# Two attention stages of a two-block transformer: dense pieces dealt in halves, a projection begun inside the attention, a division moved to GpSimd

## The chip, the cores and the metric

The kernel runs on one core of one Trainium2 chip. The metric is device time in microseconds, the median over executions; less is better. An engine is named by its short name in rows: PE is TensorE, DVE VectorE, ACT ScalarE, POOL GpSimd, SP the queue that issues loads.

## What is computed

512 tokens of width 1024 pass two transformer blocks in float32. The first block's attention has two halves whose results are concatenated and projected by `w_o`:

```python
o_nsa = nsa_attention(q_n, k_cmp, v_cmp, k_slc, v_slc, k_win, v_win, gates, nsa_slopes)
o_swa = swa_attention(q_s, k_s, v_s, sinks, swa_slopes)
mix = jnp.concatenate([o_nsa, o_swa], axis=-1) @ w_o
x = x + rmsnorm(mix, attn_post_g)
```

A gated MLP with a short convolution follows (`w_gate_up`, `w_down`), then a gated embedding term. The second block has a neighbourhood attention (8 heads) beside a retention, `w_out`, and an MLP:

```python
s = jnp.where(valid, s + bias, NEG)
p = jax.nn.softmax(s, axis=-1)
out = jnp.einsum('bhcqij,bicjhd->bcqhd', p, v_win)
x = x + jnp.concatenate([na_out, ret_out], axis=-1) @ w_out
x = x + jnp.square(jax.nn.relu(rms_norm(x, norm_mlp) @ w_up)) @ w_down
```

## The kernel before

Every engine has its own program, written out by hand, and waits on semaphores. No scheduler reorders anything.

**Dense products.** A float32 product is made of three matmuls (`triple`, lines 593 to 595): high weight by high input, high by low, low by high. A weight comes in pieces of 128x512. SP loads piece i into one of five `raw` buffers, ScalarE makes its high part `wh` (L1323), VectorE (L2022) or GpSimd (L2943) its low part `wl`, into one of five pairs. So the high part of piece i+5 waits until TensorE has finished piece i. A piece against 512 tokens is 12 matmuls with 512 columns.

**First attention.** 28 units run through a pipeline of 31 steps: units 0 to 7 are sliding window, units 8, 13, 18 and 23 the compressed branch, the others selected and window branches in turn. In step s each engine does, in this order:

- TensorE: dense pieces given to the step by `FILL1`; transpositions of unit s-2 (`turn1`, L813, or L854 for a compressed unit); scores of unit s+1 (`scores1`, L799 and L800, or L843); values of unit s-3 (`values1`, L826 and L827, L866 for the compressed part).
- VectorE: scaling of the dense piece that ended (`filled`, L2095 and L2097), mask and minimum of unit s (`soft1`, L2191), sum of the two heads of an output (`out_add`, L2214), its low part (`out_low`, L2219), low parts of the probabilities of unit s-3 (`rest1`, L2207), reciprocal for unit s-1 (`norm1`, L2272), then low parts of queries or keys (`filled_low`, L2104, L2105, L2109).
- ScalarE: copies that a finished dense piece asks for (`filled`; for a `w_o_swa` piece the copy `acc<-bank`, L1533), exponent of unit s (L1510), `wh` of a later piece, high parts of the transposed probabilities (L1516), copy of an output (L1521).
- GpSimd: division of unit s-1 with its gate (`norm1`, L2969, four instructions), then low parts of weights (L2943).

**Banks.** PSUM has eight banks. `Banks` hands them out first in, first out: `take` gives the one free for longest, and the taker waits until whoever read its former content is done. Scores, transpositions, outputs and dense results all take from this one list.

**Behind the attention.** The projection of the selected half, `w_o_nsa`, has eight pieces with four inputs each. The fourth input is the last output of the attention. `behind_last` computes inputs 0 to 2 of the first two pieces after step 30, and then input 3 of both; pieces 2 to 7 follow. As each of the eight results comes, VectorE adds it (`y1`, L2344), makes a low weight part, and adds squares for the norm (L2086). SP's queue waits for the values of the last unit, loads two quarters of `X` (L3059), waits for `y1(2)`, loads the other two, and then `praw` (L3060), which ScalarE turns into `PH` (L1601) in turn between two squares, and VectorE into `PL` (L2363). TensorE's norm sums (L724) wait for the sixth addition of squares.

**Neighbourhood attention.** Eight units, ten steps. TensorE: scores of unit s+1, values of s-2, transpositions of s-1, then one or two dense pieces (`FILL2`). VectorE: `soft` (L2191), `rest` (L2207), then `norm`, the reciprocal (L2198) and four multiplications (L2202, 1280 columns in all), then work on dense results and outputs.

## Time and profile before

| | |
|---|---|
| median of 3 runs | 1287.24 us (1286.85 to 1287.76) |
| profiled execution, its own time | 1286.42 us |
| its span, first to last instruction | 1284.5 us |
| TensorE busy | 1263.0 us, 98% |
| VectorE busy | 786.6 us, 61% |
| ScalarE busy | 647.9 us, 50% |
| GpSimd busy | 216.9 us, 17% |
| mean granted TensorE clock | 0.996 |

The profiled time is 0.8 us under the median, and its span 1.9 us under its own time. Busy shares are means over stages. The first attention's steps run from about 72 to 228 us, its projection to 250 us, the neighbourhood attention from about 827 to 895 us. In a timeline of TensorE the length given beside a matmul reaches into the next one; what a matmul costs is the distance between starts, about 0.23 us for one with 512 columns at full clock.

### The profile page before, as it was taken

How to read it: one execution, taken by the hardware profiler on the slowest of the kernel's cores; microseconds unless marked ns; L12 is line 12 of the kernel's file. 1: busy time of each engine (PE TensorE's matmuls, PEld its weight loads, DVE VectorE, ACT ScalarE, POOL GpSimd, SP SyncE). 2: the span in 40 equal slices, each digit the busy share in tenths (PEclk: the TensorE clock that was granted, in tenths of full speed). 3: DMA queues.
4: the chain of work that ended last, by engine and by line, in shares of the span. 5: the costliest groups of instructions: out<-in, count | busy, mean ns of one | idle time of the engine just before them, and what ended most of it. 6: DMA issues, size and time to landing. Idle time of an engine off the chain costs nothing.

```text
span 1284.5 us, 16448 instructions
## 1 busy us (share of the span) xinstructions
PE 1263.0 (98%) x6004; PEld 1045.6 (81%) x6004; DVE 786.6 (61%) x1465; ACT 647.9 (50%) x1261; POOL 216.9 (17%) x234
## 2 busy tenths in 40 slices
PE   9999999999999999999999999999999999999998
PEld 8887888878888888888787777887888888888887
DVE  6689687686645565356788876589644343343334
ACT  6787788554335433233555655586533252332344
POOL 0064555000100011001002101032311030110111
PEclk9998999999999999999999999999999999999999
DMA  7211110423333323332333212432333324233332
GB/s 275 86 50 34 42 41 26 170 82 99 90 100 98 98 90 99 99 96 68 115 91 98 76 56 68 131 112 68 98 99 92 97 75 118 79 115 89 100 90 67
DMA packets 64626, 118.20 MB, mean 92 GB/s; under 512 B 7713, under 2 KB 12193, under 8 KB 64289
## 3 DMA queue, kind: packets, MB, share of 16 engines
q1 hardware_dynamic: 62704, 112.86, 29.3%
q10 hardware_dynamic: 1840, 4.29, 1.1%
q8 instruction: 48, 0.79, 0.3%
q14 instruction: 34, 0.27, 0.1%
HBM read 115.02 MB, written 2.10 MB: 91 GB/s over the span
## 4 chain that ended last, share of the span: by engine, by line
PE 90%; DVE 4%; ACT 2%; issue 2%; DMA 1%; POOL 1%; POOLq 0%; SPq 0%; DVEq 0%; ACTq 0%
PE bank L593 26%; PE bank L595 25%; PE bank L594 25%; PE bank L813 2%; PE bank L693 2%; PE bank L694 2%; PE bank L695 2%; PE bank L826 1%; PE bank L827 1%; PE bank L799 1%; PE bank L800 1%; PE bank L767 1%; DVE q2p L2191 0%; DMA praw<-in_pT 0%; DVE r_bc L2086 0%
## 5 line engine op out<-in xcount | busy, mean ns | idle before, releaser
L2022 DVE TENSOR_TENSOR wl<-raw,wh 128x512 fp32r<-128x512 f32 (+2 forms) x360 | 267.5, 754 | 325.5 <-ACT wh L1323 324.8
L1323 ACT ACTIVATE wh<-raw 128x512 fp32r<-128x512 f32 (+1 forms) x398 | 242.2, 618 | 284.7 <-PE bank L595 273.7
L593 PE MATMUL bank<-AH,wh 128*128 128x512 f32 (+1 forms) x848 | 333.8, 394 | 2.1 <-DVE AL L2036 0.8
L595 PE MATMUL bank<-AH,wl 128*128 128x512 f32 (+1 forms) x848 | 329.3, 388 | 0.0
L594 PE MATMUL bank<-AL,wh 128*128 128x512 f32 (+1 forms) x848 | 327.0, 386 | 0.0
L593 PE MATMUL bank<-BH,wh 128*128 128x512 f32 x624 | 247.7, 397 | 1.6 <-ACT acc L1533 1.6
L595 PE MATMUL bank<-BH,wl 128*128 128x512 f32 x624 | 244.6, 392 | 0.0
L594 PE MATMUL bank<-BL,wh 128*128 128x512 f32 x624 | 243.0, 389 | 0.0
L595 PEld LDWEIGHTS bank<-AH,wl 128*128 128x128 f32 x848 | 159.6, 188 | 35.8
L593 PEld LDWEIGHTS bank<-AH,wh 128*128 128x128 f32 x848 | 159.9, 189 | 35.2 <-issue 2.9
L594 PEld LDWEIGHTS bank<-AL,wh 128*128 128x128 f32 x848 | 159.7, 188 | 33.0 <-issue 0.2
L593 PEld LDWEIGHTS bank<-BH,wh 128*128 128x128 f32 x624 | 117.3, 188 | 27.7 <-ACT acc L1533 2.1
L595 PEld LDWEIGHTS bank<-BH,wl 128*128 128x128 f32 x624 | 117.2, 188 | 27.2
L594 PEld LDWEIGHTS bank<-BL,wh 128*128 128x128 f32 x624 | 117.2, 188 | 25.6 <-issue 0.5
L2985 POOL TENSOR_TENSOR BL<-tmp,BH 128x512 fp32r<-128x512 f32 x22 | 28.6, 1300 | 354.4 <-ACT BH L1632 354.4
L3013 POOL TENSOR_TENSOR AL<-tmp,AH 128x512 fp32r<-128x512 f32 x32 | 40.6, 1303 | 269.6 <-ACT AH L1954 269.6
L2943 POOL TENSOR_TENSOR wl<-raw,wh 128x512 fp32r<-128x512 f32 x38 | 50.2, 1323 | 100.2 <-ACT wh L1323 100.2
L1510 ACT ACTIVATE pp<-pp,small 128x128 f32<-128x128 f32 (+2 forms) x96 | 50.2, 525 | 7.5 <-DVE small L2191 7.1
L2969 POOL TENSOR_SCALAR pp<-pp,small,gates 128x128 f32<-128x128 f32 (+1 forms) x64 | 40.9, 654 | 34.2 <-DVE small L2272 34.2
L2805 DVE TENSOR_TENSOR X<-X,bank 128x512 f32<-128x512 f32 x46 | 31.5, 686 | 24.3 <-PE bank L595 24.2
L2869 DVE SCALAR_TENSOR_TENSOR tmp<-bank,r_bc 128x512 f32<-128x512 f32 x32 | 22.0, 691 | 27.6 <-PE bank L595 16.1
L2191 DVE CUSTOM_DVE_ANT_0 pp<-bank,dn 128x512 f32<-128x512 f32 (+1 forms) x64 | 27.5, 486 | 15.9 <-PE bank L800 15.7
(332 smaller groups left out, 1617.4 us busy)
## 6 DMA issues: line engine op xcount, KB each, us to landing
raw<-in_w_dn SPq DMA_DIRECT2D x104, 256.0 KB, 2.7
raw<-in_w_gu SPq DMA_DIRECT2D x88, 256.0 KB, 2.6
raw<-in_w_up SPq DMA_DIRECT2D x64, 256.0 KB, 2.6
raw<-in_w_nsa SPq DMA_DIRECT2D x16, 256.0 KB, 2.7
raw<-in_w_pg SPq DMA_DIRECT2D x16, 256.0 KB, 2.7
raw<-in_w_naq SPq DMA_DIRECT2D x16, 256.0 KB, 2.7
nbi<-in_na_bias ACTq DMA_DIRECT2D x8, 448.0 KB, 3.4
raw<-in_w_swa SPq DMA_DIRECT2D x10, 256.0 KB, 2.7
```

The source lines that it names most:

```text
L593: t.matmul(o, w, xh, start=start, stop=False, skip_group_check=skip)
L594: t.matmul(o, w, xl, start=False, stop=False, skip_group_check=skip)
L595: return t.matmul(o, wl, xh, start=False, stop=stop, skip_group_check=skip)
L1323: a.activation(W[i % NW].h[:, 0:n], RAW[i % NRAW][:, 0:n], ACT.Copy).then_inc(*s_wh.up(i))
L1510: m = a.activation(o, o, ACT.Exp, bias=m4[:, qb:qb + 1], scale=-1.0, accum_out=s4[:, qb:qb + 1])
L2022: v.tensor_tensor(w.l[:, 0:n], RAW[i % NRAW][:, 0:n], w.h[:, 0:n], ALU.subtract).then_inc(*s_wl.up(i))
L2191: m = v.tensor_tensor_reduce(o, b[:, col:col + w], bias(qb), scale, init, ALU.add, ALU.min, m4[:, qb:qb + 1])
L2805: v.tensor_tensor(chunk(X, c), chunk(X, c), bank.ap(key)[:, :], ALU.add).then_inc(*s_sv.up(done))
L2943: g.tensor_tensor(w.l[:, 0:n], RAW[i % NRAW][:, 0:n], w.h[:, 0:n], ALU.subtract).then_inc(*s_wlg.up(i))
L2969: g.tensor_scalar(o, o, r, by, ALU.mult, ALU.mult).then_inc(*s_nmg.up((u, qb)))
L2985: g.tensor_tensor(x.l, tmp.ap(("u", k))[:, 0:T], x.h, ALU.subtract).then_inc(*s_xlg.up(("ff", k)))
L3013: g.tensor_tensor(x.l, tmp.ap(("rs", 8 * gi + k))[:, 0:T], x.h, ALU.subtract).then_inc(*s_xlg.up(("up", 8 * gi + k)))
```

## The change

Three edits.

1. **First attention's dense pieces.** The table `FILL1` becomes `PARTS1`, which gives a piece to a step whole (`ALL`), or its first or last two inputs (`FRONT`, `BACK`). `part` takes these halves. `("w_nsa", 3)`, the second half of the window keys, moves from step 8 to step 7, which had none; query pieces `("w_nsa", 10)` to 13 begin a step earlier; pieces 14 and 15 are spread over steps 13 to 16, the `w_o_swa` pieces over steps 16 to 27 rather than in 13, 14, 18, 21, 23, 26 and 27. `FILL1` is kept as the table of where a piece ends, and the other engines follow it.
2. **The projection.** `out_front` computes inputs 0 to 2 of one piece; it is called in steps 28, 29 and 30, ahead of the values, and once behind step 30. `out_back` computes input 3, for pieces 0 to 3 one after the other; whole pieces 4 to 7 follow. The neighbourhood attention's `w_out_na` uses the same functions in the order it had.
3. **The division.** `norm` leaves VectorE. Its reciprocal for unit s-1 now stands at the head of VectorE's step s, ahead of `soft`; the four multiplications are on GpSimd, with a second factor of one, ahead of its low weight parts. TensorE's transpositions wait for GpSimd's semaphore.

```diff
-FILL1 = {0: [("w_swa", 6), ("w_swa", 7)], 1: [("w_swa", 8)], 2: [("w_nsa", 0), ("w_swa", 9)], 3: [("w_nsa", 1)],
-         4: [("w_nsa", 8)], 5: [("w_nsa", 9)], 6: [("w_nsa", 2)], 8: [("w_nsa", 3)], 9: [("w_nsa", 10)],
-         10: [("w_nsa", 11)], 11: [("w_nsa", 12)], 12: [("w_nsa", 13)], 13: [("w_o_swa", 0)],
-         14: [("w_o_swa", 1), ("w_o_swa", 2)], 15: [("w_nsa", 14)], 16: [("w_nsa", 15)], 18: [("w_o_swa", 3)],
-         21: [("w_o_swa", 4)], 23: [("w_o_swa", 5)], 26: [("w_o_swa", 6)], 27: [("w_o_swa", 7)]}
+ALL, FRONT, BACK = (0, 1), (0,), (1,)
+PARTS1 = {0: [("w_swa", 6, ALL), ("w_swa", 7, ALL)], 1: [("w_swa", 8, ALL)], 2: [("w_nsa", 0, ALL), ("w_swa", 9, ALL)],
+          3: [("w_nsa", 1, ALL)], 4: [("w_nsa", 8, ALL)], 5: [("w_nsa", 9, ALL)], 6: [("w_nsa", 2, ALL)], 7: [("w_nsa", 3, ALL)],
+          8: [("w_nsa", 10, ALL)], 9: [("w_nsa", 11, ALL)], 10: [("w_nsa", 12, ALL)], 11: [("w_nsa", 13, FRONT)],
+          12: [("w_nsa", 13, BACK)], 13: [("w_nsa", 14, FRONT)], 14: [("w_nsa", 14, BACK)], 15: [("w_nsa", 15, FRONT)],
+          16: [("w_nsa", 15, BACK), ("w_o_swa", 0, FRONT)], 17: [("w_o_swa", 0, BACK), ("w_o_swa", 1, FRONT)],
+          18: [("w_o_swa", 1, BACK)], 19: [("w_o_swa", 2, FRONT)], 20: [("w_o_swa", 2, BACK), ("w_o_swa", 3, FRONT)],
+          21: [("w_o_swa", 3, BACK)], 22: [("w_o_swa", 4, ALL)], 23: [("w_o_swa", 5, FRONT)], 24: [("w_o_swa", 5, BACK)],
+          25: [("w_o_swa", 6, ALL)], 26: [("w_o_swa", 7, FRONT)], 27: [("w_o_swa", 7, BACK)]}
+FILL1 = {s: [(name, i) for name, i, h in parts if 1 in h] for s, parts in PARTS1.items()}
...
+            def out_front(name, c, src, ready, key):
+
+                b, free = bank.take((key, c))
+                w, i = weights(name, c)
+                e.wait_ge(*free)
+                for k in range(3):
+                    e.wait_ge(ready(k))
+                    col = slice(P * k, P * k + P)
+                    triple(b[:, :], w.h[:, col], src[k].h, src[k].l, w.l[:, col], k == 0, False)
...
+                if s >= N_UNITS:
+                    out_front("w_o_nsa", s - N_UNITS, B, nsa_out, "wo")
                 if s >= 3:
                     values1(s - 3)
...
-            behind_last("w_o_nsa", B, nsa_out, "wo")
-            for c in range(2, 8):
+            out_front("w_o_nsa", 3, B, nsa_out, "wo")
+            for c in range(4):
+                out_back("w_o_nsa", c, B, nsa_out, "wo")
+            for c in range(4, 8):
                 product("w_o_nsa", c, B, nsa_out, [0, 1, 2, 3], 1, 4, [("wo", c)])
...
             for s in range(10):
+                if 1 <= s <= 8:
+                    s4 = S4[(s - 1) % 6]
+                    e.wait_ge(s_ex.at(("na", s - 1)))
+                    v.reciprocal(s4, s4).then_inc(*s_nm.up(("r", ("na", s - 1))))
                 if s < 8:
...
-                if 1 <= s <= 8:
-                    norm(NA, ("na", s - 1), PP2[(s - 1) % 2], S4[(s - 1) % 6])
...
+            def norm(L, u, pp, s4, by):
+                e.wait_ge(s_nm.at(("r", u)))
+                for qb in range(4):
+                    o = pp[:, L["off"][qb]:L["off"][qb] + L["w"][qb]]
+                    g.tensor_scalar(o, o, s4[:, qb:qb + 1], by(qb), ALU.mult, ALU.mult).then_inc(*s_nmg.up((u, qb)))
...
-            for s in range(10):
-                for name, i in FILL2.get(s, ()):
+            for s in range(1, 11):
+                if s <= 8:
+                    norm(NA, ("na", s - 1), PP2[(s - 1) % 2], S4[(s - 1) % 6], one)
+                for name, i in FILL2.get(s - 1, ()):
                     lo(WHERE[name, i] + 4)
```

How the order moves on the engines, at three places. Line numbers behind the change are those of its own code.

VectorE in the first attention, where the low parts of the window keys (`kb_wn`) are made. Before, at the end of step 9, behind the compressed unit's division:

```order
L2260 TENSOR_REDUCE small<-pc 128x8
L2262 RECIPROCAL small<-small 128x8
L2264 TENSOR_TENSOR small<-small,gates 128x8
L2266 TENSOR_TENSOR pc<-pc,small 128x2x4x31
L2104 TENSOR_TENSOR kb_wn_95<-tmp_74,ka_wn_94 64x512
L2105 TENSOR_TENSOR kb_wn_95<-tmp_74,ka_wn_94 64x512
L2104 TENSOR_TENSOR kb_wn_97<-tmp_74,ka_wn_96 64x512
L2105 TENSOR_TENSOR kb_wn_97<-tmp_74,ka_wn_96 64x512
L2191 ISA pp_111,small<-bank,dn 128x512
```

Now at the end of step 8, behind the small compressed values (`vc`), and ahead of the mask of unit 9:

```order
L2276 TENSOR_TENSOR small<-small 128x4
L2278 RECIPROCAL small<-small 128x4
L2334 TENSOR_TENSOR vc_104<-bank,vc_104 31x64 x2
L2334 TENSOR_TENSOR vc_105<-bank,vc_105 31x64 x2
L2118 TENSOR_TENSOR kb_wn_95<-tmp_74,ka_wn_94 64x512
L2119 TENSOR_TENSOR kb_wn_95<-tmp_74,ka_wn_94 64x512
L2118 TENSOR_TENSOR kb_wn_97<-tmp_74,ka_wn_96 64x512
L2119 TENSOR_TENSOR kb_wn_97<-tmp_74,ka_wn_96 64x512
L2205 ISA pp_115,small<-bank,dn 128x512
```

The four low parts moved up by one step, ahead of the mask of unit 9 instead of that of unit 10.

TensorE in step 29, from the transpositions of the last unit on. Before, the values of unit 26 follow at once:

```order
L813 MATMUL bank<-ident,pp_115 128x128 x10
L866 MATMUL bank<-pct,vc_105 128x512
L826 MATMUL bank<-pth_107,v_100 128x512
L827 MATMUL bank<-ptl_108,v_100 128x512
L826 MATMUL bank<-pth_107,v_101 128x384
```

Now the front of projection piece 1 stands between (nine matmuls, the first five shown):

```order
L818 MATMUL bank<-ident,pp_115 128x128 x10
L598 MATMUL bank<-BH,wh_60 128x512
L599 MATMUL bank<-BL,wh_60 128x512
L600 MATMUL bank<-BH,wl_61 128x512
L598 MATMUL bank<-BH,wh_60 128x512
L599 MATMUL bank<-BL,wh_60 128x512
```

Steps 28 and 30 have the same for pieces 0 and 2, so 27 matmuls moved ahead of the last values.

VectorE in the neighbourhood attention, step 2. Before, the division stands between the low parts of the probabilities and the scaling of a dense result:

```order
L2207 TENSOR_TENSOR p2l_161<-bank,p2h_160 128x512
L2207 TENSOR_TENSOR p2l_161<-bank,p2h_160 128x384 x2
L2198 RECIPROCAL small<-small 128x4
L2202 TENSOR_SCALAR q2p_165<-q2p_165,small 128x256
L2202 TENSOR_SCALAR q2p_165<-q2p_165,small 128x384 x2
L2202 TENSOR_SCALAR q2p_165<-q2p_165,small 128x256
L2095 TENSOR_TENSOR tmp_74<-bank,r_bc 128x512
```

Now the scaling follows at once:

```order
L2213 TENSOR_TENSOR p2l_161<-bank,p2h_160 128x512
L2213 TENSOR_TENSOR p2l_161<-bank,p2h_160 128x384 x2
L2109 TENSOR_TENSOR tmp_74<-bank,r_bc 128x512
L2711 TENSOR_TENSOR nkb_184<-tmp_74,nka_183 64x512
L2712 TENSOR_TENSOR nkb_184<-tmp_74,nka_183 64x512
```

and GpSimd has the multiplications ahead of its low weight parts:

```order
L2972 TENSOR_SCALAR q2p_164<-q2p_164,small,ones 128x256
L2972 TENSOR_SCALAR q2p_164<-q2p_164,small,ones 128x384 x2
L2972 TENSOR_SCALAR q2p_164<-q2p_164,small,ones 128x256
L2951 TENSOR_TENSOR wl_59<-raw_51,wh_58 128x512
L2951 TENSOR_TENSOR wl_61<-raw_52,wh_60 128x512
```

## Rows read from the trace of the kernel before

**Rows 1.** The page, busy time by engine (share of the span, instructions).

```profile
PE 1263.0 (98%) x6004; PEld 1045.6 (81%) x6004; DVE 786.6 (61%) x1465; ACT 647.9 (50%) x1261; POOL 216.9 (17%) x234
```

**Rows 2.** TensorE's waits, 96 to 245 us: total us, times, longest us.

```profile
PE bank L813 <- ACT acc L1533: 2.9, 3, 1.3
PE bank L593 <- ACT acc L1533: 1.6, 2, 1.3
PE bank L799 <- issue: 1.6, 1, 1.6
PE bank L813 <- POOL pp L2969: 1.1, 2, 0.6
```

**Rows 3.** TensorE's timeline, steps 7 and 8: start us, length, instruction, [idle before, releaser].

```profile
101.04 1.51 PE L813 MATMUL bank<-ident,pp 128*128 128x128 f32 x6 [0.64 <-POOL pp L2969]
102.94 0.33 PE L790 MATMUL bank<-cw,chid 128*64 128x64 f32 x2 [0.39 <-DVE os L2214]
...
107.58 0.63 PE L595 MATMUL bank<-AH,wl 128*128 128x512 f32 x1
108.00 0.63 PE L593 MATMUL bank<-AH,wh 128*128 128x512 f32 x1
...
110.36 0.39 PE L593 MATMUL bank<-AH,wh 128*128 128x512 f32 x1
110.59 0.39 PE L594 MATMUL bank<-AL,wh 128*128 128x512 f32 x1
```

**Rows 4.** TensorE's timeline, window keys in step 9.

```profile
119.27 0.47 PE L799 MATMUL bank<-ka_wn,qs 128*128 128x512 f32 x1 [1.58 <-issue]
```

**Rows 5.** By stretch: length, busy PE, PEld, DVE, ACT, POOL (x), clock, DMA.

```profile
105.10:137.18 32.08, 30.50 (x172) 26.69 (x173) 28.62 (x76) 25.26 (x68) 15.25 (x21) 0.92 0.13 38
836.00:896.00 60.00, 58.21 (x321) 48.96 (x321) 54.01 (x137) 44.76 (x107) 17.13 (x13) 1.00 0.31 94
```

**Rows 6.** ScalarE's timeline, steps 13 and 14.

```profile
144.94 0.59 ACT L1521 ACTIVATE os<-bank 64x512 f32<-64x512 f32 x1 [1.85 <-PE bank L827]
145.56 0.60 ACT L1533 ACTIVATE acc<-bank 128x512 f32<-128x512 f32 x1
```

**Rows 7.** Chain that ended last, 237 to 251 us: start us, us, what.

```profile
236.81 0.70 DVE ACC L2344
...
238.38 5.71 DMA praw<-in_pT
...
244.11 0.64 ACT PH L1601
...
249.85 0.70 DVE r_bc L2086
...
250.69 0.41 PE bank L724 x2
```

**Rows 8.** VectorE's timeline: the attention's last output, first projection result.

```profile
230.57 0.69 DVE L2219 TENSOR_TENSOR BL<-os,BH 128x512 fp32r<-128x512 f32 x1 [0.70 <-ACT BH L1525]
233.38 0.69 DVE L2344 TENSOR_TENSOR ACC<-bank,acc 128x512 f32<-128x512 f32 x1 [2.12 <-PE bank L595]
```

**Rows 9.** Timelines of the neighbourhood attention: TensorE, then VectorE and GpSimd.

```profile
868.40 0.39 PE L799 MATMUL bank<-nka,nq 128*128 128x256 f32 x1 [1.05 <-DVE os L2214]
870.73 0.35 PE L826 MATMUL bank<-p2h,v 128*128 128x256 f32 x1 [0.55 <-DVE p2l L2207]
...
860.27 1.27 DVE L2202 TENSOR_SCALAR q2p<-q2p,small 128x256 f32<-128x256 f32 x4
866.07 1.68 DVE L2219 TENSOR_TENSOR AL<-r_bc,AH 128x512 fp32r<-128x512 f32 x1
...
865.51 1.68 POOL L2943 TENSOR_TENSOR wl<-raw,wh 128x512 fp32r<-128x512 f32 x1 [2.14 <-ACT wh L1323]
```

**Rows 10.** GpSimd's timeline, divisions of the first attention's wide units.

```profile
136.29 2.38 POOL L2969 TENSOR_SCALAR pp<-pp,small,gates 128x128 f32<-128x128 f32 x4 [2.27 <-DVE small L2272]
141.92 3.30 POOL L2969 TENSOR_SCALAR pp<-pp,small,gates 128x128 f32<-128x128 f32 x4 [1.99 <-DVE small L2272]
```

More of the change, by code:

```diff
@@ L641, in product, with part @@
                         group(name, k0 + s // kpp, bs, keys, src, ready, ks[s:s + kpp], s == 0, s + kpp == n, fresh is not None)
-            def part(name, k, src, ready, ks, key, first, last, between=None):
-                if first:
+            def part(name, k, src, ready, ks, key, first, last, between=None, halves=ALL):
+                if first and 0 in halves:
                     b, free = bank.take(key)
@@ L649, in part @@
                 w, i = weights(name, k)
-                for j in range(4):
+                for j in range(2 * halves[0], 2 * halves[-1] + 2):
                     x = src[ks[j]]
@@ L1216, in na_out @@
                 return s_xl.at(("ob", "na", k))
-            behind_last("w_out_na", A, na_out, "xo")
+            for c in range(2):
+                out_front("w_out_na", c, A, na_out, "xo")
+            for c in range(2):
+                out_back("w_out_na", c, A, na_out, "xo")
             for c in range(2, 8):
@@ L2194, in soft @@
                     bank.read(("sc", u, i), (s_sf, ("b", u, i)))
-            def norm(L, u, pp, s4):
-                e.wait_ge(s_ex.at(u))
-                v.reciprocal(s4, s4).then_inc(*s_nm.up(("r", u)))
-                e.wait_ge(s_nm.at(("r", u)))
-                for qb in range(4):
-                    o = pp[:, L["off"][qb]:L["off"][qb] + L["w"][qb]]
-                    v.tensor_scalar(o, o, s4[:, qb:qb + 1], None, ALU.mult).then_inc(*s_nm.up((u, qb)))
             def rest(L, u, pt, before):
@@ L2958, in gpsimd, with one @@
             g.memset(chid[1][:, :], 0.0).then_inc(*s_z.up("zero"))
+            def norm(L, u, pp, s4, by):
[3 more added lines that the diff above has]
+                    g.tensor_scalar(o, o, s4[:, qb:qb + 1], by(qb), ALU.mult, ALU.mult).then_inc(*s_nmg.up((u, qb)))
+            def one(qb):
+                return ones[:, 0:1]
             def norm1(u):
[L2961 to L2964 removed]
+                if unit(u)[0] == "swa":
+                    norm(SWA, u, probs(u), S4[u % 6], one)
+                else:
                     e.wait_ge(s_dv.at("gv"))
[L2966 to L2969 removed]
+                    norm(NSA, u, probs(u), S4[u % 6], lambda qb: gate_of(u)[:, qb:qb + 1])
             for s in range(1, N_UNITS + 3):
```

44 lines of the change are left out of this document (14 added, 30 removed).

## The prediction

> **What bounds the kernel now.** I read busy time by engine first: TensorE is busy 1263.0 of 1284.5 us [rows 1]. The change adds and removes no matmul; only TensorE's waits and its slow clock can go, so 21 us of idle and the little that the clock costs are all there is. TensorE's waits of the first attention come next [rows 2]. Three kinds matter: 4.5 us on `acc`, the copy of a `w_o_swa` result out of its bank; 1.6 us ahead of the window keys' scores; 1.1 us on GpSimd's division. The timeline shows more than the waits do, since matmul lengths there overlap the next start. In step 7, with no dense piece, the seven transpositions of unit 5 began at 100.07 and what followed them at 102.94 [rows 3]; elsewhere such a group takes 0.7, so 2.2 were lost. Behind that thin stretch the granted clock fell to its lower level, 1.2 GHz: starts of 512-column matmuls stand 0.42 apart at 107.58, and 0.23 again at 110.36 [rows 3]. The slow stretch begins behind 102.94 and ends ahead of 110.36, 6.9 us at half speed by the starts, 3.4 lost. The scores at 119.27 had TensorE idle for 1.58 [rows 4], 1.8 by starts. The stretches show who stands behind this: from the mask of unit 8 to that of unit 13 (105.10 to 137.18) VectorE is busy 28.62 of 32.08, and in the neighbourhood attention 54.01 of 60 [rows 5].
>
> **First attention, steps 7 to 13.** The removed stalls are 2.2 + 3.4 + 1.8 = 7.4 us, and that is the upper end. TensorE could do less: from its 30.50 busy us [rows 5] the new table takes one piece out of steps 8 to 12 (12 x 0.23 = 2.7), and the slow clock inflated them by some 2.5, so it needs 25.3. VectorE needs the same 28.6, and its work can hardly start earlier: with `w_nsa` 3 in step 7, TensorE reaches unit 8's scores at about 103.8 instead of 103.2, now at full clock, and the mask starts at 105.05 instead of 105.10. So VectorE sets the pace, and TensorE waits for it in small portions. If it idles 1.4 us in handovers instead of 3.5, unit 13's mask comes at 135.1 instead of 137.18: lead 2.1, the lower end. Placing the steps one by one with the durations of the rows, TensorE enters step 13 at 134.5 instead of 138.3, with the same pieces done; it waits less behind VectorE's last work. I take **3.8**, nearest to this placement. The window keys are no wait any more: their low parts are ready at 114.2, wanted at 114.6.
>
> **First attention, steps 13 to 27.** A result's bank is taken again as the next step's first bank, while ScalarE copies the ended unit's output (0.59) and only then `acc` (0.60) [rows 6]: 1.3 us wherever an output ended in that step, 0.3 elsewhere. Following the list of banks, five such waits (1.3, 1.3, 1.3, 0.3, 0.3) become three (step 19 behind `w_o_swa` 1, 1.3; steps 22 and 25, 0.3); the others meet a `BACK` half, which takes no bank. That gives 4.5 - 1.9 = **2.6**, between 0 (all come back elsewhere, as VectorE's read of a score bank in step 17 might) and 4.5. Sum of the first attention 6.4.
>
> **Projection.** In steps 28 to 30 the fronts (9 x 0.23 = 2.07 each) fill the 1.0 us that TensorE lost on GpSimd's last division (the 1.1 of rows 2). Against that, front 1 takes the bank of an output read 1.5 us after its values, 0.5 lost; and only front 3 (2.07) now stands between the last values and input 3, which came 2.9 us after them (the first matmul behind the values started at 228.35, the low part ended at 231.26) [rows 8], 0.85 lost. Before, two fronts of 4.1 covered it. So TensorE ends the eight pieces no earlier, 29.7 us after step 28 began as against 29.6.
>
> What matters is what comes late. The first result came at 233.38 [rows 8], 12.6 us into this stretch; now four come in a bunch, from 16.7 on. VectorE takes them one by one: result, low part, result, low part, squares, result, some 4.0 us to the end of `y1(2)`, at 20.7 instead of 16.6. On `y1(2)` SP's queue releases the second half of `X` and then `praw`, which needed 5.71 us from issue to landing, and on which ScalarE waited [rows 7]. From its landing at 244.11 a chain of VectorE and ScalarE work without a gap led to the last addition at 249.85 and to TensorE's norm sums at 250.69 [rows 7]; TensorE had finished its pieces at 250.4, so nothing was to spare. The transfer carries 1.5 MB, and nothing in the change makes that shorter. So the whole chain moves by 4.05, and TensorE stands idle about 4 us ahead of the norm sums: **-4.0**, between 0 (if `praw` lands early) and -4.5.
>
> An idle stretch like this costs clock too. In step 7 a stretch with 2.2 of 2.9 us idle was enough for the fall, which cost 3.4 [rows 3]. Here it would meet norm sums and embedding matmuls, part of them hidden behind VectorE: I take **-2.0**, between 0 and -3.4.
>
> **Neighbourhood attention.** VectorE gives up four multiplications of 1.27 together, eight times [rows 9]; GpSimd takes 2.38 to 3.30 for 1280 columns in the first attention [rows 10], and had been busy 17 of 60 us here [rows 5]; its 8 x 2.4 to 3.3 = 19 to 26 us fit. The division starts before the mask instead of behind it and the probabilities' low parts (2.0 + 1.6), so it is done at about 2.7 to 3.5 us into VectorE's step instead of 5.1. TensorE's path there is VectorE: at 868.40 it waited for an output sum, at 870.73 for low parts [rows 9]. Idle, by that view, is 1.8 of 60 [rows 5]; by starts it is more, as in step 7: 132 dense matmuls at 0.23 and 22 groups of scores, values and transpositions of 1.0 to 1.2 make 55.3 of the 60.5 us from 835.0 to 895.5, so 5.2 are lost. Relieved of 1.27 per step of 6 to 9 us, VectorE falls below TensorE: I take **+4.2**, between 0.5 and 5.2. The reciprocal now waits for ScalarE's exponent with the next mask behind it; 3.0 us of low parts, additions and sums stand between mask and reciprocal, the exponent takes 2.2, so it costs nothing.
>
> A rule speaks against this edit. The Trainium skill, GPSIMD Engine Reference, section "Key points", says that GpSimd shares its SBUF interfaces with VectorE, and that they contend when VectorE reads two SBUF inputs. The trace agrees: `AL`, 0.69 elsewhere, took 1.68 at 866.07 beside a GpSimd subtraction begun at 865.51 [rows 9]. Whether a division, with one input, does as much no row tells here; that is the third rival.
>
> **Sum.** 3.8 + 2.6 + 0 - 4.0 - 2.0 + 4.2 = 4.6 us from the profiled 1286.4, so 1281.8. The median stood 0.8 higher: 1287.2 - 4.6 = 1282.6, rounded **1282.5**.
>
> **Rivals.** (A) The tail has no wait: `praw` lands in time, or the chain is shorter than I hold. Then 10.6 are gained, **1276.6**. For it: VectorE had idle stretches before `y1(4)`; against: ScalarE's wait for the transfer is in the chain. (B) VectorE's pace swallows steps 7 to 13, and one `acc` wait returns: 2.1 + 1.3 - 6.0 + 4.2 = 1.6, **1285.6**. (C) Slower: GpSimd's added work holds up VectorE's two-input operations. With four per step at up to 1 us, 1.27 saved per step can be outweighed; it decides from one and a half collisions per step. Then the neighbourhood attention gives 0.5 at best or loses 2, and with the pace of B and the full fall of the clock in the tail: 2.1 + 1.3 - 7.4 - 2 = -6, **1293**. (D) The halves do not do what they say: TensorE's waits move to score banks in steps 17 and 20 and to the divisions, which have 1.4 instead of 2.7 us of cover. First attention gains 2 in all: 2 - 6 + 4.2 = 0, **1287**.
>
> **How the numbers follow.** My forecast has 0.45, A 0.17, B 0.14, C 0.12, D 0.12. 0.2% of the time, 2.6 us, is about what a measurement of this kernel can tell from none; so faster means under 1284.7. The forecast lies there for nine tenths, A whole, B a third: 0.63. Slower is C: 0.11. The rest, 0.26, is within. The range leaves out half of A's low side and most of C: 1276.5 to 1288.
>
> **What would show it.** Right: no idle at about 100 to 103 and no slow clock behind it; no wait ahead of the window keys; one `acc` wait of 1.3 and two of 0.3; VectorE busy over 90% in steps 8 to 12; about 4 us idle before the norm sums (L729 then), with `praw` in the chain and landing some 27 us behind step 28's transpositions; the neighbourhood attention's TensorE waits under 0.5. Wrong, if the norm sums wait under 1 us, if the clock falls in steps 9 to 14, or if VectorE's low parts of keys take over 1 us beside GpSimd's divisions.

## The result and the profile after

| | before | changed |
|---|---|---|
| median | 1287.05 us (4 runs, 1286.27 to 1287.76) | 1301.87 us (4 runs, 1299.92 to 1302.81) |
| ratio, 95% interval | | 1.0113 [1.0098, 1.0128] |
| profiled execution, its span | 1286.42, 1284.5 | 1302.53, 1300.7 |

The change made the kernel 14.8 us slower. The forecast was 4.6 faster; the time lies outside its range and 9 us above its slowest rival.

The page's busy times of the changed kernel, to compare with [rows 1]:

```profile
PE 1267.9 (97%) x6004; PEld 1050.6 (81%) x6004; DVE 782.5 (60%) x1433; ACT 647.6 (50%) x1261; POOL 236.3 (18%) x266
```

The work is the same; TensorE is busy 4.9 us longer, with a mean granted clock of 0.992 instead of 0.996, and idle 11 us longer. Its waits from 96 to 262 us, against [rows 2] (total us, times, longest us):

```profile
PE bank L729 <- DVE r_bc L2100: 5.4, 1, 5.4
PE bank L598 <- ACT acc L1547: 3.5, 2, 2.2
PE bank L818 <- DVE vc L2334: 2.8, 1, 2.8
PE bank L818 <- POOL pp L2972: 1.4, 4, 0.4
PE bank L848 <- DVE ptl L2213: 1.4, 1, 1.4
PE bank L818 <- DVE os L2220: 0.9, 2, 0.5
PE bank L831 <- DVE ptl L2213: 0.7, 1, 0.7
PE bank L598 <- DVE BL L2225: 0.7, 1, 0.7
PE bank L598 <- DVE os L2220: 0.4, 1, 0.4
```

Of five waits for `acc` two are left, where three were forecast, but one of them takes 2.2 us, and behind that one the granted clock fell, which it did nowhere in these steps before:

```profile
185.00:206.00 21.00, 18.76 (x109) 16.03 (x108) 12.65 (x38) 14.93 (x44) 10.86 (x15) 0.92 0.14 39
```

The wait ahead of the window keys is gone. In their place stand waits on banks that VectorE reads (`vc`, `ptl`, `os`), and 5.4 us ahead of the norm sums. The same stretches as [rows 5], placed by the same masks and steps (length, busy PE, PEld, DVE, ACT, POOL, clock, DMA):

```profile
107.30:138.70 31.40, 26.30 (x159) 22.30 (x158) 29.01 (x74) 25.35 (x67) 16.85 (x20) 1.00 0.14 43
848.00:908.00 60.00, 55.64 (x302) 47.95 (x301) 47.92 (x106) 44.44 (x109) 32.35 (x40) 0.94 0.29 87
```

In the first TensorE's need fell from 30.5 to 26.3 us, at full clock, and yet the stretch is only 0.7 shorter. In the second VectorE is 6 us less busy and GpSimd 15 more, and TensorE, whose clock fell, does fewer matmuls in 60 us.

Both traces, cut at the same instructions of TensorE:

| stretch | before | changed | difference | forecast |
|---|---|---|---|---|
| start to the 7th step's dense piece or transpositions | 100.1 | 101.8 | +1.8 | 0 |
| to step 13 | 38.3 | 37.7 | -0.6 | -3.8 |
| to step 28 | 82.4 | 83.7 | +1.2 | -2.6 |
| to the norm sums | 29.9 | 37.1 | +7.2 | +4.0 |
| to the neighbourhood attention's start | 576.5 | 579.1 | +2.65 | +2.0 |
| to the end | 457.4 | 461.3 | +3.9 | -4.2 |

Every row but the first was a term of the sum; plus is slower here. All five came out worse, the fourth by little.

### The profile page after: what moved, and what is told of

Read it like the earlier page. It is cut to its first block, busy times and chain, and to the rows that moved or that the text cites. A ratio compares the mean times of both kernels' runs of the same rounds, so it can differ in the third digit from the quotient of the medians.

```text
span 1300.7 us, 16451 instructions
## 1 busy us (share of the span) xinstructions
PE 1267.9 (97%) x6004; PEld 1050.6 (81%) x6004; DVE 782.5 (60%) x1433; ACT 647.6 (50%) x1261; POOL 236.3 (18%) x266
## 4 chain that ended last, share of the span: by engine, by line
PE 87%; DVE 6%; ACT 3%; issue 2%; DMA 1%; POOL 0%; SPq 0%; POOLq 0%; DVEq 0%; ACTq 0%
PE bank L598 25%; PE bank L600 24%; PE bank L599 24%; PE bank L698 2%; PE bank L699 2%; PE bank L700 2%; PE bank L818 2%; PE bank L831 1%; PE bank L832 1%; PE bank L804 1%; PE bank L805 1%; ACT q2p L1524 1%; DMA raw<-in_w_ple 1%; DVE q2p L2205 1%; PE bank L772 1%
## 5 line engine op out<-in xcount | busy, mean ns | idle before, releaser
L2811 DVE TENSOR_TENSOR X<-X,bank 128x512 f32<-128x512 f32 x46 | 31.5, 687 | 24.8 <-PE bank L600 24.7
L2972 POOL TENSOR_SCALAR pp<-pp,small,ones 128x256 f32<-128x256 f32 (+1 forms) x32 | 22.1, 703 | 80.0 <-DVE small L2278 80.0
```

What stands on the lines that cost most here:

```text
L2811: v.tensor_tensor(chunk(X, c), chunk(X, c), bank.ap(key)[:, :], ALU.add).then_inc(*s_sv.up(done))
L2972: g.tensor_scalar(o, o, s4[:, qb:qb + 1], by(qb), ALU.mult, ALU.mult).then_inc(*s_nmg.up((u, qb)))
```

## The experiments

Each kernel below was compared with the kernel before on one chip, in five rounds (`d0_before` ran once). A distance "8 to 13" is from the first compressed score of unit 8 to that of unit 13, the tail is from step 28 to the norm sums.

### The three edits alone

The diff of each is the part of the change that its name says, on the kernel before.

`a1_table`:

> The kernel before with the new table of dense pieces alone (PARTS1 and halves in part); projection and division as before. Theory T (the losses stand in separate stages and add): the two traces differ by +0.6 us from step 7 to step 28 where the removed stall of step 7 was to give 6; so this kernel comes out within 1.5 us of the kernel before (1286 to 1289), with a wait of 2 to 3 us of the transpositions in step 8 for VectorE's read of the compressed values, and none in step 7. Rival R (the table is sound, its gain is eaten by the other two edits): 1281 to 1283.

`a2_proj`:

> The kernel before with the projection's fronts in steps 28 to 30 alone. Theory T: the tail of the first attention and its norm carry +7.2 and +2.65 us of the loss by the two traces; so 1295 to 1298, with an idle stretch of 5 us ahead of the norm sums and a granted clock that falls behind it. Rival R (the old table leaves the tail's transfers early enough, the loss comes only with the new table's late pieces of w_o_swa): 1287 to 1291. Rival C (the prediction's size): 4.05 + 2 us, 1293.

`a3_div`:

> The kernel before with the neighbourhood attention's division on GpSimd alone, reciprocal at the head of VectorE's step. Theory T: +3.9 us by the two traces, so 1290 to 1292. Rival N (this stage's loss in the trace of the change was inherited from what stood ahead of it): 1283 to 1287.

| | median, before beside it (us) | ratio, interval | 8 to 13 | 13 to norm sums | norm sums to neighbourhood attention | to the end |
|---|---|---|---|---|---|---|
| before | | | 32.9 | 114.6 | 576.5 | 457.4 |
| changed | 1301.87, 1287.05 | 1.0113 [1.0098, 1.0128] | 31.5 | 123.1 | 579.1 | 461.3 |
| `a1_table` | 1290.16, 1287.91 | 1.0022 [1.0013, 1.0031] | 31.5 | 118.0 | 576.6 | 457.4 |
| `a2_proj` | 1294.69, 1287.91 | 1.0054 [1.004, 1.0067] | 32.9 | 119.0 | 579.0 | 457.4 |
| `a3_div` | 1290.53, 1287.91 | 1.0026 [1.0016, 1.0035] | 32.9 | 115.0 | 576.4 | 460.9 |

No edit gains, each loses in the stage that it touches, and the losses add: 2.3 + 6.8 + 2.6 = 11.7 of 14.8 by the medians. By the spans, less what each trace shows ahead of step 7's first instruction (next experiment), it is 3.0 + 6.9 + 4.1 = 14.0 of 14.4. `a1_table` came out 1.2 us above what theory T gave it, `a2_proj` 0.3 under, nearer to T than to C (1293). The rivals by which an edit was sound by itself fall. The table has two losses. Between 13 and 28 it is 1.3 us slower, with the same wait of 2.2 us for `acc` in step 22 and a fall of the clock behind it at 191.1 us, as in the changed kernel. And its tail is 32.0 against 29.9: behind half a piece in steps 26 and 27, instead of a whole one, TensorE waits 1.0 us for GpSimd's divisions and 0.7 for VectorE's low parts, where it waited 0.4 and nothing. These two readings come from the waits; no run changed either place by itself.

### What the traces differ by before any changed instruction

`d0_before`:

> The kernel before once more, for a second profile. In the traces so far TensorE's clock rises at either of two points at the start of the program, and unit 8's scores begin at 103.2 to 103.8 or at 104.8 to 105.1 us. Theory L (this is the execution's luck and no effect of an edit): this one may show either, and its own time is 1285.5 to 1286.5 with the early and 1287.5 to 1289 with the late one, everything behind in the same distances. Rival K (each kernel has its own): the early one again.

It took 1288.3 us, and its unit 8 began at 104.8 instead of 103.2. TensorE's timeline at the start, in the first profile of the kernel before and then in this one (start us, length, instruction):

```profile
5.66 0.99 PE L680 MATMUL bank<-wh,AH 128*128 128x408 f32 x4 [1.04 <-ACT wh L1323]
6.48 0.91 PE L683 MATMUL bank<-wh,AL 128*128 128x408 f32 x4
```

```profile
5.68 1.70 PE L680 MATMUL bank<-wh,AH 128*128 128x408 f32 x4 [0.87 <-ACT wh L1323]
7.18 1.56 PE L683 MATMUL bank<-wh,AL 128*128 128x408 f32 x4
```

The same four matmuls take 0.8 us or 1.5, from start to start: the clock rises earlier or later, and in `d0_before` everything behind keeps its distances. The changed kernel's trace has the late rise too. So theory L holds, and 1.8 of the 16.2 us of span belong to the execution. It isn't the only such chance: in `e1_low_waits`, below, the clock fell once more at 765 us, 3.5 us after sixteen matmuls of one column each had begun, without a wait of TensorE and in code that no edit touches (length, busy PE, PEld, DVE, ACT, POOL, clock, DMA):

```profile
762.00:770.00 8.00, 8.00 (x37) 6.43 (x38) 5.22 (x19) 4.50 (x7) 0.00 (x0) 0.79 0.11 33
```

Its stretch from the norm sums to the neighbourhood attention took 578.1 us for that, not 576.5. So a difference of 1 or 2 us is read from the medians and from single stretches, not from the length of one trace.

### Steps 7 to 13

`a4_key7` moves one entry on the kernel before:

```diff
-6: [("w_nsa", 2)], 8: [("w_nsa", 3)], 9: [("w_nsa", 10)],
+6: [("w_nsa", 2)], 7: [("w_nsa", 3)], 9: [("w_nsa", 10)],
```

> The kernel before with one entry moved: the second half of the window keys in step 7 instead of 8, nothing in step 8. Theory T (the new table's loss is its query pieces begun a step early, which hand the transpositions of step 8 the bank of the compressed values; moving the one piece keeps step 7 busy and the clock up): 1281 to 1284. Rival V (VectorE sets the pace of these steps, whatever TensorE does): 1285 to 1287. Rival S (step 8 is now the thin one, and the stall and the clock's fall move there): 1286 to 1289.

1289.35, ratio 1.0015 [1.0006, 1.0024]. The stall of step 7 is gone, and in step 8 the scores of unit 9 wait for `vc`; 8 to 13 took 33.3:

```profile
111.93 0.80 PE L799 MATMUL bank<-ka_sl,qs 128*128 128x512 f32 x1 [5.04 <-DVE vc L2328]
```

It is nearest to rival S: the stall and the clock's fall moved to step 8. What S did not name is the cause, the list of banks: the key's bank comes back a step sooner, so another taker gets the bank of the compressed values, and VectorE reads that one last in its step. Here the taker is the scores of unit 9. In the changed kernel it is the transpositions of unit 6; TensorE's row and VectorE's:

```profile
113.87 0.55 PE L818 MATMUL bank<-ident,pp 128*128 128x128 f32 x3 [2.83 <-DVE vc L2334]
```

```profile
112.91 0.91 DVE L2334 TENSOR_TENSOR vc<-bank,vc 31x64 fp32r<-31x64 f32 x4 [0.49 <-ACT vc L1581]
```

`b1_key7_vc` adds, and `c1_table_vc` has on `a1_table`:

```diff
-                bank.give(("vc",))
...
+                if s == 8:
+                    bank.give(("vc",))
```

> The window keys' second half in step 7, and the bank of the compressed values given back to the list behind step 8's scores instead of at once. Theory T (in the kernel with the one piece moved, 5.0 us of idle stand in step 8 only because the transpositions of unit 6 get that bank, which VectorE reads at 111 us; all other steps run in the same distances): that wait goes, the slow clock behind it too, and the time falls by the 5 to 7 us that the old table lost at steps 7 to 9: 1281 to 1284. Rival V (VectorE sets the pace between the masks of unit 8 and 13): TensorE then waits elsewhere, 1285 to 1288.

> The new table alone, and the bank of the compressed values given back to the list behind step 8's scores. Theory T (the table's own losses are separate: 2.8 us of wait for that bank in step 8; 2.2 us of wait for ScalarE's copy of an output result in step 22; 2.1 us in the thinned last steps): 1287 to 1288.5, that is 1.5 to 3 us under the run with the table alone. Rival V (VectorE sets the pace in steps 8 to 12, the wait only moves): 1289.5 to 1290.5, no change.

`b1_key7_vc` gave 1287.84, ratio 1.0005 [0.9996, 1.0014]; `c1_table_vc` 1289.93, 1.0019 [1.001, 1.0028], as `a1_table`. The wait for `vc` went and others came: in `b1_key7_vc` TensorE waits 2.4 and 1.2 us for `os`, the sum of outputs on VectorE. Theory T falls in both, V stands. `d3_key_twice` gives more work to VectorE alone:

```diff
+                if key[1] == "wn":
+                    v.tensor_tensor(dst.l[half(g), 0:n], t[half(g), 0:n], dst.h[half(g), 0:n], ALU.subtract).then_inc(*s_ql.up((*key, g, "once")))
+                    e.wait_ge(s_ql.at((*key, g, "once")))
                 v.tensor_tensor(dst.l[half(g), 0:n], t[half(g), 0:n], dst.h[half(g), 0:n], ALU.subtract)
```

> The run with the keys in step 7 and the bank given later, where VectorE makes one low part of the window keys twice (twice 0.69 us or more, at the end of its step 8). Theory V (VectorE sets the pace between the masks of unit 8 and 13): the distance from unit 8's to unit 13's compressed scores grows from 31.6 to 33.0 or more, and the time from 1287.8 to 1289.2 to 1290. Rival E (TensorE's own waits set it, VectorE has 2.6 us idle there): 31.6 and 1287.8, no change.

1289.96, ratio 1.0019 [1.001, 1.0028]: 0.0014 over `b1_key7_vc`, 1.8 us for 1.4 us of added work. The two intervals overlap a little; but all eleven times of `d3_key_twice` (1289.1 to 1291.7) lie above all eleven of `b1_key7_vc` (1285.9 to 1288.5), with the kernel before at 1287.64 and 1287.22 beside them. Its waits of TensorE, 96 to 140 us:

```profile
PE bank L812 <- DVE os L2218: 4.0, 1, 4.0
PE bank L798 <- DVE os L2218: 1.2, 1, 1.2
```

These waits prove nothing by themselves: `d1_all`, below, has the same instructions in these steps as `b1_key7_vc`, without the added work, and waits 4.0 and 1.2 us as well. Nor do the distances 8 to 13: 31.6 in `b1_key7_vc`, 34.1 in `d1_all`, 34.8 in `d3_key_twice`. The clock differs between the three traces. In `b1_key7_vc` it was low once, ahead of the long wait (0.57 from 112 to 116 us); in `d1_all` at the wait and behind it (0.62, then 0.53, from 116 to 124), where it cost time; in `d3_key_twice` on both sides (0.68 from 112 to 116 and again from 120 to 124). So the times, over eleven runs each, decide for V over E; how much of the 1.8 us is the clock's stays open.

### The waits for acc

`c3_acc_early`, on the kernel before, ScalarE's program:

```diff
                 for name, i in later:
-                    filled(name, i)
+                    if name != "w_o_swa":
+                        filled(name, i)
...
+                for name, i in FILL1.get(s, ()):
+                    if name == "w_o_swa":
+                        filled(name, i)
                 if 3 <= s < N_UNITS + 3 and closes(s - 3):
```

> The kernel before, ScalarE copies the result of a w_o_swa piece (acc) in the step in which TensorE makes it, ahead of its copy of the ended unit's output, instead of behind it at the head of the next step. Theory A (TensorE's 4.5 us of waits for acc are real idle, as the prediction took them; 2.6 of them were a term of its sum): the waits vanish from the trace and the time falls by 2.5 to 4.5 us, 1282.7 to 1284.7. Rival P (TensorE is held by VectorE and GpSimd right behind, the wait only moves to the outputs' sum or the division): 1286 to 1287.5.

1286.76, ratio 0.9994 [0.9986, 1.0003]; 13 to norm sums 114.5 against 114.6. TensorE's waits, 96 to 245 us, against [rows 2]:

```profile
PE bank L799 <- issue: 1.6, 1, 1.6
PE bank L813 <- POOL pp L2973: 1.6, 4, 0.6
PE bank L813 <- DVE os L2218: 1.5, 2, 1.0
PE bank L790 <- DVE os L2218: 0.4, 1, 0.4
PE bank L854 <- DVE pc L2270: 0.4, 2, 0.2
```

All 4.5 us on `acc` are gone, and no gain can be told from none (by the interval at most 1.8 us). In step 14 TensorE came 1.6 us ahead. From step 19 on, which has no dense piece, it lost that bit by bit to GpSimd's division and VectorE's `os` (0.8 ahead at unit 22's scores, nothing at unit 27's). The `acc` waits had stood in front of those. That is rival P.

### The projection

`b2_proj_sp`, on `a2_proj`, SP's queue:

```diff
                 if c == 2:
+                    d.dma_start(praw[:, :], ins["pT"]).then_inc(*s_p.up("in", by=16))
+                    load(WHERE["w_ple", 1])
                     e.wait_ge(s_sv.at(("y1", 2)))
...
-            d.dma_start(praw[:, :], ins["pT"]).then_inc(*s_p.up("in", by=16))
```

> The projection's fronts alone, as in the run before, with SP's queue in another order: praw and the second piece of w_ple are issued ahead of the wait for y1(2), the second half of X behind it. Theory T (the projection's loss of 6.8 us is the chain y1(2), X, praw, w_ple, ScalarE, squares, norm sums): most of it goes, with it the idle stretch of 5 us ahead of the norm sums and the slow clock behind: 1287 to 1290. Rival B (the bunch of four results is itself what is late: eight additions, low parts and squares of VectorE from 241 us on): 1291 to 1294, the norm sums wait for VectorE at the same place. Rival D (the transfer is as slow wherever it is issued): no change against 1294.7.

1289.52, ratio 1.0013 [1.0004, 1.0022], 5.2 us under `a2_proj` by the medians and 3.9 by the two traces behind unit 8's first score. The wait ahead of the norm sums, first in `a2_proj`, then here:

```profile
PE bank L724 <- DVE r_bc L2095: 4.2, 1, 4.2
```

```profile
PE bank L724 <- DVE r_bc L2095: 1.2, 1, 1.2
```

Tail 34.3, 31.3, and 29.9 before. Theory T holds for three of the four microseconds of wait; the last 1.2 are rival B's: in this trace the chain ahead of the norm sums is VectorE's additions, low parts and squares, and no transfer. The changed kernel's chain of waits shows what lands last, against [rows 7]:

```profile
245.19 0.61 DVE ACC L2350
...
247.14 0.43 SPq L3076
...
247.61 7.98 DMA raw<-in_w_ple
255.62 0.64 ACT wh L1337
...
259.47 0.70 DVE r_bc L2100
...
260.31 1.73 PE bank L729 x7
```

It is not `praw` (5.71 us from issue to landing before, 6.24 now) but a load queued behind it, the second piece of `w_ple`: 7.98 us under way, where the trace of the kernel before has 6.64 for the same load. ScalarE makes its high part ahead of the sixth square. Behind the wait the clock is low:

```profile
264.71 0.63 PE L600 MATMUL bank<-PH,wl 128*128 128x512 f32 x1
265.14 0.63 PE L598 MATMUL bank<-PH,wh 128*128 128x512 f32 x1
...
266.55 0.40 PE L599 MATMUL bank<-PL,wh 128*128 128x512 f32 x1
266.78 0.40 PE L600 MATMUL bank<-PH,wl 128*128 128x512 f32 x1
```

Starts stand 0.43 apart, then 0.23: the two levels, 1.2 and 2.4 GHz, as in [rows 3].

### The neighbourhood attention

VectorE's groups in the changed kernel, 839 to 912 us, and then the kernel before, 827 to 895 (busy us, mean ns, idle before, releaser):

```profile
L2715 DVE TENSOR_TENSOR nq<-tmp,nq 64x512 fp32r<-64x512 f32 x4 | 6.3, 1585 | 3.4 <-ACT nq L1835 3.3
L2712 DVE TENSOR_TENSOR nkb<-tmp,nka 64x512 fp32r<-64x512 f32 x4 | 4.8, 1190 | 0.1
L2711 DVE TENSOR_TENSOR nkb<-tmp,nka 64x512 fp32r<-64x512 f32 x4 | 4.1, 1028 | 3.1 <-ACT nka L1832 3.1
L2839 DVE RECIPROCAL small<-small 128x4 f32<-128x4 f32 x8 | 1.4, 171 | 2.5 <-ACT q2p L1524 2.4
```

```profile
L2705 DVE TENSOR_TENSOR nkb<-tmp,nka 64x512 fp32r<-64x512 f32 x4 | 3.1, 784 | 1.5 <-ACT nka L1818 1.4
L2706 DVE TENSOR_TENSOR nkb<-tmp,nka 64x512 fp32r<-64x512 f32 x4 | 2.7, 686 | 0.1
L2709 DVE TENSOR_TENSOR nq<-tmp,nq 64x512 fp32r<-64x512 f32 x4 | 2.7, 686 | 1.5 <-ACT nq L1821 1.4
```

VectorE got rid of 12.5 us of multiplications. It gives 6.7 back in these twelve low parts (6.3 + 4.8 + 4.1 instead of 3.1 + 2.7 + 2.7), and waits 3.5 more for ScalarE's copies that they need. The mask of 128x384, which ran beside the divisions, takes 550 ns in both. So in this stage it is not the division that collides but GpSimd's low weight parts: VectorE, early now, waits for ScalarE to end the exponent and a `wh`, and starts 0.5 us after GpSimd starts on that `wh`. Eight of the twelve are lengthened, and each of the eight ends 0.55 us behind the end of the GpSimd subtraction that it met.

The division only met nothing here that it could collide with. In the first attention of the kernel before it does meet low parts, of the queries, and that is why [rows 10] has 3.30 us for it beside 2.38. VectorE's row at that place:

```profile
141.85 1.54 DVE L2109 TENSOR_TENSOR qs<-tmp,qs 64x512 fp32r<-64x512 f32 x2
```

The first two of the four divisions of 141.92 take 0.94 and 0.98 us, and VectorE's second low part 0.83 instead of 0.69.

Once in this stage VectorE was late enough that TensorE stood still, and the clock fell:

```profile
884.60 0.58 PE L804 MATMUL bank<-nka,nq 128*128 128x256 f32 x1 [3.70 <-DVE os L2220]
884.97 0.42 PE L805 MATMUL bank<-nkb,nq 128*128 128x256 f32 x1
```

Three edits of `a3_div`. `b3_div_recip`, VectorE:

```diff
             for s in range(10):
-                if 1 <= s <= 8:
-                    s4 = S4[(s - 1) % 6]
-                    e.wait_ge(s_ex.at(("na", s - 1)))
-                    v.reciprocal(s4, s4).then_inc(*s_nm.up(("r", ("na", s - 1))))
...
                     rest(NA, ("na", u), PT2[u % 2], [s_pv.at(("na", u - 2))] if u >= 2 else [])
+                if 1 <= s <= 8:
+                    s4 = S4[(s - 1) % 6]
+                    e.wait_ge(s_ex.at(("na", s - 1)))
+                    v.reciprocal(s4, s4).then_inc(*s_nm.up(("r", ("na", s - 1))))
```

`b4_div_wh`, ScalarE:

```diff
-                    hi(WHERE[name, i] + 4)
...
                     turned(NA, ("na", u), PT2[u % 2], [s_pv.at(("na", u - 2))] if u >= 2 else [s_pv.at(("r", 3, 3))])
+                for name, i in later:
+                    hi(WHERE[name, i] + 4)
```

`e1_low_waits`, GpSimd:

```diff
                     norm(NA, ("na", s - 1), PP2[(s - 1) % 2], S4[(s - 1) % 6], one)
+                    e.wait_ge(s_th.at((("na", s - 1), 2)))
```

> The neighbourhood attention's division on GpSimd, but its reciprocal stands on VectorE where it stood before, behind the low parts of the probabilities. Theory W (the reciprocal at the head of the step makes VectorE wait 2.4 us for ScalarE's exponent with the mask behind it): 1287 to 1289. Theory G (the loss is the low parts of keys and queries, stretched beside GpSimd's weight parts, 6.7 us busy, and the waits for ScalarE's copies): no gain, the division starts later, 1290 to 1293.

> The neighbourhood attention's division on GpSimd as changed, and ScalarE makes the high parts of the later weight pieces at the end of its step, behind its copies of queries, keys, outputs and transposed probabilities, instead of between them. GpSimd's low parts then start later, away from VectorE's low parts of keys and queries. Theory G: VectorE's nq and nkb low parts take 0.68 each again instead of 1.2 to 1.6, its waits for ScalarE's copies shrink by 0.6 each: 1283 to 1287, the gain that the division's move was to bring. Rival W (reciprocal): 1289 to 1291. Rival H (the weights' high parts come too late for TensorE): above 1292.

> The neighbourhood attention's division on GpSimd as changed, ScalarE's order as it was, and GpSimd makes its low weight parts only when ScalarE has copied the transposed probabilities of the step's unit. Theory P (the loss is GpSimd's low parts beside VectorE's low parts of queries and keys): their lengths fall from 1.6 and 1.2 to about 0.7 us, and the time to about that of the run with ScalarE's late high parts, 1287.5 to 1289. Rival S (that run gained because ScalarE's copies came 0.6 us earlier): 1290 to 1291, VectorE waits for nq and nka as before.

| | median, before beside it | ratio, interval | stage to the end |
|---|---|---|---|
| `a3_div` | 1290.53, 1287.91 | 1.0026 [1.0016, 1.0035] | 460.9 |
| `b3_div_recip` | 1290.42, 1287.22 | 1.0025 [1.0016, 1.0034] | 461.1 |
| `b4_div_wh` | 1288.17, 1287.22 | 1.0003 [0.9994, 1.0013] | 457.7 |
| `e1_low_waits` | 1288.12, 1287.86 | 1.0007 [0.9998, 1.0015] | 458.0 |

The reciprocal's place costs nothing (theory W falls). `b4_div_wh` is 2.4 us under `a3_div`, though not down to the 1283 to 1287 of its theory. Delaying GpSimd's low parts is enough, whether by ScalarE's order or by a wait on GpSimd alone. In `e1_low_waits`, 827 to 900 us:

```profile
L2701 DVE TENSOR_TENSOR nq<-tmp,nq 64x512 fp32r<-64x512 f32 x4 | 2.7, 686 | 2.8 <-ACT nq L1821 2.7
```

Its wait for ScalarE is nearly what it was, its length is not. Theory P of that run stands. Both stay level with the kernel before, not under it: with the collisions gone TensorE waits for the divisions, 2.7 us in seven waits in `e1_low_waits`.

### Repairs together, and a version that beats both

`c2_repaired` is the changed kernel with the edits of `b1_key7_vc` (bank), `b2_proj_sp` and `b4_div_wh`. `c4_wh_late` is the kernel before, its division on VectorE, with only ScalarE's edit of `b4_div_wh`. `d1_all` adds to it `b1_key7_vc` and `c3_acc_early`, `e2_wh_acc` only `c3_acc_early`. `d2_wh_both` is `c4_wh_late` and the same order in the first attention:

```diff
-                for name, i in later:
-                    behind(name, i)
                 if 2 <= s <= N_UNITS + 1:
...
+                for name, i in later:
+                    behind(name, i)
                 later = FILL1.get(s, ())
```

> The changed kernel with three small repairs: the bank of the compressed values given back later, praw and the second piece of w_ple issued ahead of the wait for y1(2), and ScalarE's high weight parts at the end of its steps in the neighbourhood attention. Theory T (the change's loss is these three mechanisms, and they add): 1301.9 less 1.5 to 3, less 5.2, less 2.3 gives 1291 to 1293. Rival I (with fronts and thin last steps together, VectorE's bunch of results is late whatever the transfers do): 1294 to 1297.

> The kernel before, its division on VectorE, with ScalarE's high weight parts at the end of its steps in the neighbourhood attention. Theory G (ScalarE's copies of queries and keys are what VectorE waits for, 3 us, and GpSimd's low parts stretch VectorE's twice): 1 to 3 us less, 1284.5 to 1286.5. Rival D (only the moved division made these two meet; with it on VectorE they are apart already): 1287 to 1288.

> The kernel before with every repair that touches the two attentions: window keys in step 7 with the bank given later, acc copied in its own step, high weight parts at the end of ScalarE's steps in the neighbourhood attention. Theory V (the first attention is paced by VectorE and the removed waits only covered others): no better than the last of these alone, 1284 to 1286. Rival A (small gains of the first attention add once the waits of both kinds are gone): 1282 to 1284.

> The kernel before with ScalarE's high weight parts at the end of its steps in both attentions. Theory G (ScalarE's copies reach VectorE and TensorE 0.6 us earlier where it is behind, and GpSimd's low parts start later): 1283 to 1285, as good as or better than 1284.95. Rival H (in the first attention GpSimd divides first, so its low parts are late already and now meet VectorE's low parts of queries and keys): 1286 to 1289.

> The kernel before with ScalarE's high weight parts at the end of its steps in the neighbourhood attention, and acc copied in the step that makes it. Theory A (the two are in separate stages and each gives what it gave alone, 2.1 and 0.5 us): 1284.3 to 1285.3. Rival M (the second was noise): 1285 to 1286, not better than the first alone.

| | median, before beside it | ratio, interval |
|---|---|---|
| `c2_repaired` | 1293.26, 1287.55 | 1.0044 [1.003, 1.0058] |
| `c4_wh_late` | 1284.95, 1287.55 | 0.9984 [0.9975, 0.9993] |
| `d1_all` | 1286.41, 1287.64 | 0.9991 [0.9982, 1.0] |
| `d2_wh_both` | 1287.96, 1287.64 | 0.9998 [0.9987, 1.0008] |
| `e2_wh_acc` | 1285.48, 1287.86 | 0.9984 [0.9975, 0.9993] |

`c2_repaired` came out 0.3 us above theory T's range: 5.7 us of loss are left, above all a 13 to norm sums of 118.8, with step 22's wait for `acc` of 2.2 us and the clock's fall behind it still there. `c4_wh_late` beats both kernels and is 2.6 us under the one before; its stage to the end is 455.3 against 457.4, and TensorE's wait of 1.05 us for `os` at 868.40 [rows 9] is gone. The low part `AL`, 1.68 us in [rows 9], no longer meets GpSimd; the group before, then in `c4_wh_late` (827 to 895 us):

```profile
L2219 DVE TENSOR_TENSOR AL<-r_bc,AH 128x512 fp32r<-128x512 f32 x2 | 2.4, 1177 | 0.0
```

```profile
L2220 DVE TENSOR_TENSOR AL<-r_bc,AH 128x512 fp32r<-128x512 f32 x2 | 1.4, 686 | 0.0
```

Its rival D, that only the moved division made the two meet, falls. Two things moved at once, ScalarE's copies earlier and GpSimd's subtractions later; which of them gave how much of the 2.6 us no run separates. The early `acc` adds nothing to it (rival M), and `d1_all`, above both its ranges, is no better than it alone. In the first attention the same order is no gain: `d2_wh_both` has the time of its rival H and 117.8 from 13 to the norm sums, but not by H's mechanism. VectorE's four low parts of queries behind unit 13 take 3.0 us together in its trace as in the one before. What its trace shows is a wait for `acc` in step 14 of 1.8 us instead of 1.3 and a granted clock of 0.79 behind it, from 144 to 152 us.

## Why the prediction was wrong, step by step

The figures in this section are gains: plus is faster.

- **Steps 7 to 13 (+3.8 forecast, 0.6 measured).** The failing step is the lower bound, and with it the placement above it: "if it idles 1.4 us in handovers instead of 3.5" took VectorE's idle as removable. It idled 2.4 (31.4 less 29.01), and its work grew by 0.4. And of the banks only those of dense pieces had been followed, not the list as a whole: that missed the wait of 2.8 us for `vc`. Seeing it would have won nothing (`c1_table_vc`): VectorE sets the pace there, which was rival B, and even 2.1 was too much.
- **Steps 13 to 28 (+2.6 forecast, -1.2 measured).** Three waits for `acc` were to be left, of 1.9 us; there are two, of 3.5. The one of step 19 came at 1.3 as forecast, the one of step 25 is gone, but step 22 waited 2.2, not 0.3, because ScalarE reached that `acc` only behind an exponent, a `wh`, three transposed parts and `BH`. Behind it the clock fell, to 0.92 in the mean of 185 to 206 us, a term that the sum had at nothing; by these figures it cost up to 1.7 us, an estimate (0.08 of 21 us). The larger error is of kind: a wait was priced at its length. `c3_acc_early` removes all five, and 13 to norm sums stays at 114.5 against 114.6, since they stand in front of waits for VectorE and GpSimd.
- **The tail (-4.0 forecast, -7.2 measured).** The mechanism was right: results in a bunch, `y1(2)` late, transfers late, idle ahead of the norm sums. The term was mis-sized: missed were the table's part, 2.0 (thin steps 26 and 27; `a1_table`), and the last load of the queue, 7.98 us instead of 6.64, which had not been in the chain. A reading was wrong too, without changing the sum: `praw` carries 512 KB; 1.5 MB is that with the two quarters of `X` ahead of it. Rival A, 0.17, was far off.
- **The clock behind it (-2.0 forecast, -2.65 measured).** Right in mechanism and place.
- **Neighbourhood attention (+4.2 forecast, -3.9 measured).** Rival C's mechanism, at 0.12, with the place wrong: here GpSimd's low weight parts collide, not the division. It was priced by four operations per step and "one and a half collisions"; eight low parts in the whole stage, 6.7 us longer together, and 3.5 us of waits for ScalarE were enough. That no row told what a division does was a misreading: the 3.30 us of [rows 10] were such a collision, and mostly at GpSimd's expense. The forecast's step was "relieved of 1.27 per step, VectorE falls below TensorE": VectorE's next input came from ScalarE, which had not become faster, so part of the relief became idle and the rest moved VectorE's low parts onto GpSimd's. The rule of the Trainium skill, GPSIMD Engine Reference, section "Key points", that GpSimd and VectorE contend for SBUF when VectorE reads two SBUF inputs, is borne out by the low parts (two such inputs, for `nq` 686 and now 1585 ns in the mean). Under it the mask, with one bank and one SBUF input, should be untouched, and it was, at 550 ns.
- **The reciprocal at no cost.** Right (`b3_div_recip`), though VectorE waits 2.4 us for it once, at 844.9 us, ahead of its second mask.
- **The chances.** The loss lies 9 us beyond the slowest rival. The likeliest case took for granted that three sound gains add. Each stood on a removed wait or relieved engine, and none asked which engine was next. The cases should have allowed for all three edits losing in their own stages at once.

## What to carry to other kernels

A wait has the price of its length only if nothing stands right behind it. Before it is counted, ask when TensorE would meet the next thing, or take it away alone: the five waits for `acc` lasted 4.5 us, and without them the stretch was 0.1 us shorter. Where banks or buffers come from one list, moving one entry deals the whole list out anew, so follow every taker for a few steps. And an engine relieved of work runs into its next supplier, and its work moves in time, here onto GpSimd's subtractions. One reordering on ScalarE gained 2.6 us, where moving 12.5 us of work to another engine lost 2.6.

## What the runs showed of the hardware

- Two executions of one program differ in when TensorE's clock first rises: four first matmuls took 0.8 or 1.5 us, the rest of the trace shifted by 1.6 us (`d0_before`, 1288.3 against 1286.42). The clock also fell without a wait: 0.79 from 762 to 770 us in `e1_low_waits`, TensorE busy 8.00 of 8.00 us, in part with matmuls of one column, where the trace of the kernel before shows 1.00.
- The same low part of 64x512 took 686 ns alone and 1364 to 1807 where it met GpSimd's subtraction (`a3_div`), whose own length stayed at 1.3 us; each ended 0.55 us behind that subtraction. Where the subtraction began while a low part was running, and another followed, both grew: `AL` and the subtraction took 1.68 us each [rows 9].
- GpSimd's four multiplications, 2.38 us, lengthened no mask and weren't lengthened by one; beside two low parts of queries they took 3.30 us [rows 10].
- What a fall of the clock costs depends on where it comes: with the same instructions in steps 8 to 12 it was low ahead of the wait in `b1_key7_vc` (0.57 from 112 to 116 us) and for longer, at the wait and behind it, in `d1_all` (0.62 and 0.53 from 116 to 124), and the stretch took 31.6 or 34.1 us.
